# A third row buffer in front of the DOWN stage, and eight more unsplit units in the MID stage, of a one-core decoder block with PEER retrieval

## The chip, the cores and the metric

The kernel runs on one core of a Trainium2 chip. The metric is the device time of one launch in microseconds (us), lower is better; the median over several launches is compared.

## What is computed

One decoder block on 256 tokens of width 2048: a mixer (differential attention beside a causal convolution), then a feed-forward part that looks up single-neuron experts. Only the second part matters here:

```python
def peer_ffn(h, w_q, k1, k2, u_tab, v_tab):       # 256 tokens, 16384 experts, D = 2048
    q = (h @ w_q).reshape(T, 8, 256)              # 8 heads
    s1, s2 = q[..., :128] @ k1.T, q[..., 128:] @ k2.T
    v1, i1 = top_k(s1, 16); v2, i2 = top_k(s2, 16)
    top, pos = top_k(v1[:, None] + v2[None, :], 16)   # 16 experts for each head and token
    idx, g = i1 * 128 + i2 at pos, softmax(top)
    act = gelu(einsum('thkd,td->thk', u_tab[idx], h)) * g
    return einsum('thk,thkd->td', act, v_tab[idx])
```

All of it is float32.

## The kernel before

**Two ways to one sum.** The first 192 tokens take the dense way: TensorE multiplies their activations with the whole table u (128 blocks of 128 experts, 1 MB each), a gelu follows, a matrix of gates ("weights", in DRAM, filled by small accumulating DMAs) picks what counts, and the stage DOWN multiplies with the whole table v. For the last 64 tokens the 16 chosen experts of 8 heads are gathered as rows: 64 gathers ("rows" from here on) of 128 lines of 8 KB each, 1 MB per gather, first from u and later from v.

**Stages.** The dense part runs in the stages UP, MID, THIRD and LAST over u (32 blocks each, in 4 passes of 8 blocks, the first pass written out and the other three in a hardware loop), then DOWN over v. A block is two units of 8 k-chunks. A *split* unit is done in two parts of reduced-precision products: ScalarE rounds the unit to `w_hi` (L713), VectorE makes the rest `w_low` (L1382), TensorE runs eight matmuls with `w_hi` (L1008) and eight with `w_low` (L1015). A *plain* unit goes to TensorE as it is (L1001, sixteen records for eight matmuls), with no work on ScalarE or VectorE. Only MID has plain units, six of the sixteen in each pass (j = 1, 3, 7, 9, 11, 15). MID is also the last stage in which VectorE selects the top 16 (`experts`).

**Blocks of u and v.** SyncE brings them into `raw`, a ring of four blocks (L352): block b is asked for when both units of block b-4 are used (`split_used`). `w_hi` has two buffers; ScalarE fills one when TensorE has done the `w_hi` matmuls of the split unit two before (`hi_used`).

**Rows of u.** GpSimd issues the gathers (L491) into `got[0]` and `got[1]`, which the code takes in turn; the gather of row n waits for `row_used` n-1, that is for row n-2 to be done with. Behind each gather it issues the small DMAs that add gates to `weights` (`put_weights`, L506): 4, 4 and 3 in turn behind rows 1 to 15, and 2, 2, 2, 2, 1 in turn behind the later ones. VectorE takes each row's dot product with the token in two halves (L1403) between its `w_low` units (`dots_at`, called from `lo`): 4 rows in a pass of MID (16 in all), 6 in a pass of THIRD and of LAST (48 in all). A half waits for the row's DMA (`row_in`), and everything behind it in VectorE's order waits with it.

**The turn to DOWN.** SyncE, in the callback `weights_first`, behind the first block of v: waits for all `weights_put`, then loads the first two groups of gates back (`weights_group`, L390, 384 KB each) into `weights_in[0]` and `weights_in[1]`, two tiles of their own. The further blocks of v are behind that in its order. VectorE multiplies the first group into the activations (`make_group`, L1846), ScalarE and VectorE split it (L918, L1853, L1855), and only then can DOWN's first matmul run (L1339). The same wait for `row_used` 63 and 64 stands on GpSimd in front of the first two rows of v.

Of the kernel before, what the change touches and what calls it, by code (L numbers as in the profile page):

```python
# [6 lines left out]
P = 128  # L7
D = 2048
T = 256
TD = 192  # L10
# [20 lines left out]
UNIT = 1024  # L31
# [5 lines left out]
EXPERT_BLOCKS = KEYS  # L37


def at(i, step, first):  # L40

    return first if i is None else i * step + first
# [28 lines left out]

PH_WQ = Phase(None, BLOCKS // 4, 8)
PH_UP = Phase(PH_WQ, EXPERT_BLOCKS // 32, 16, groups=tuple(range(22, 30)))
PH_MID = Phase(PH_UP, EXPERT_BLOCKS // 32, 16, plain=(1, 3, 7, 9, 11, 15), groups=(30, 31, 4, 11, 12, 13, 14, 15))
PH_THIRD = Phase(PH_MID, EXPERT_BLOCKS // 32, 16, groups=(5, 6, 7, 8, 9, 10, 16, 17))
PH_LAST = Phase(PH_THIRD, EXPERT_BLOCKS // 32, 16, groups=(0, 1, 2, 3, 18, 19, 20, 21))
PH_DOWN = Phase(PH_LAST, EXPERT_BLOCKS // 8, 16)
U_ORDER = [4 * g + i for ph in (PH_UP, PH_MID, PH_THIRD, PH_LAST) for i in range(4) for g in ph.groups]
assert sorted(U_ORDER) == list(range(EXPERT_BLOCKS))
# [18 lines left out]
B_END = B_UP + EXPERT_BLOCKS  # L98
GROUPS = EXPERT_BLOCKS // 4
ROWS = PEER_HEADS * TOPK // SLICES  # L100
DOTS_MID_FIRST, DOTS_MID = tuple(range(8, 16)), (1, 2, 5, 6, 9, 10, 13, 14)
DOTS_ROUTE = (0, 1, 3, 4, 5, 6, 8, 9, 11, 12, 13, 14)
N_MID, N_ROUTE = len(DOTS_MID) // 2, len(DOTS_ROUTE) // 2
DOT_ROWS = {PH_MID: 0, PH_THIRD: N_MID * PH_MID.n, PH_LAST: N_MID * PH_MID.n + N_ROUTE * PH_THIRD.n}
assert DOT_ROWS[PH_LAST] + N_ROUTE * PH_LAST.n == ROWS and N_MID % 2 == N_ROUTE % 2 == 0
PUTS_SECOND, PUTS_FIRST = PEER_HEADS * TOPK // 2, PEER_HEADS * TOPK
PUTS = PUTS_SECOND + PUTS_FIRST
HEAD_ROWS = ROWS // PEER_HEADS
# [11 lines left out]
ALU = mybir.AluOpType  # L120
# [4 lines left out]
def build_block(nc, x, c, c_row, w_ada, w_gate_f, b_cols, g_cols, rows, w_front, lambdas, g_subln, conv_w,  # L125
                conv_vecs, peer_wq, peer_keys, peer_u, u_rows, peer_v, v_rows, out):
    with ExitStack() as ctx:
        def sb(name, shape, dt=F32):
            return ctx.enter_context(nc.sbuf_tensor(name, shape, dt))

        def sem(name):
            return ctx.enter_context(nc.semaphore(name))
# [8 lines left out]
        def region(start, *shape):  # L141
            n = int(math.prod(shape))
            v = big[:, start:start + n]
            if len(shape) == 2:
                v = v.rearrange("p (a b) -> p a b", b=shape[1])
            if len(shape) == 3:
                v = v.rearrange("p (a b c) -> p a b c", b=shape[1], c=shape[2])
            return v
# [36 lines left out]
        h_tok = region(28672, D)  # L185
# [27 lines left out]
        with nc.sbuf_tensor("early", [P, 5 * D], F32) as early:  # L213
# [12 lines left out]
        got = [region(24576 + n * D, D) for n in range(2)] + [early[:, 3072 + n * D:3072 + (n + 1) * D] for n in range(2)]  # L226
# [17 lines left out]
        put = sel[:, 0:2 * PUTS].rearrange("p (m n) -> p m n", m=2)  # L244
        put_at = sel[:, 0:PUTS].bitcast(U32)
        put_gate = sel[:, PUTS:2 * PUTS]
        weights_in = (sb("weights_in0", [P, 4, TD]), sb("weights_in1", [P, 4, TD]))
        token = sb("token", [P, 2])
        row_info = sb("row_info", [P, 2, ROWS])
        row_gate, row_ix = row_info[:, 0, :], row_info[:, 1, :].bitcast(U32)  # L250
        dots, row_act = sb("dots", [P, ROWS]), sb("row_act", [P, ROWS])
        dots_now = sb("dots_now", [P, N_ROUTE, 2])
        pair = sel[:, 2 * PUTS:2 * PUTS + TD]
        low = sb("low", [P, TD], F32R)
        ident_r = sb("ident_r", [P, P], F32R)
# [59 lines left out]
        at_made = sem("at_made")  # L315
        twice_made, h_turned, h_tok_made = sem("twice_made"), sem("h_turned"), sem("h_tok_made")
        picked_ready, row_info_in = sem("picked_ready"), sem("row_info_in")
        row_in = [sem(f"row_in{n}") for n in range(2)]
        v_row_in = [sem(f"v_row_in{n}") for n in range(4)]
        row_used, v_row_used, dots_put, row_gelu, row_act_made = (sem("row_used"), sem("v_row_used"), sem("dots_put"),  # L320
                                                                  sem("row_gelu"), sem("row_act_made"))
# [20 lines left out]
        def _(sp):  # L342
# [44 lines left out]
            def weights_group(g, i):  # L387

                src = weights[:, bass.ds(at(i, 8 * TD, 4 * TD * g), 4 * TD)]
                sp.dma_start(weights_in[g % 2][:, :, :].rearrange("p a t -> p (a t)"), src)\  # L390
                    .then_inc(weights_back[g % 2], 16)

            def weights_first(j, i):

                if j == 1:
                    sp.wait_ge(weights_put[0], 16 * PUTS_FIRST)
                    sp.wait_ge(weights_put[1], 16 * PUTS_SECOND)
                    weights_group(0, None)
                    weights_group(1, None)
                if j == 11:  # L400
                    sp.wait_ge(at_made, 1)
                    weights_group(2, None)
# [31 lines left out]
            for it in range(PH_WQ.n):  # L434
                bring(PH_WQ, it or None, peer_wq, 0, gate_loads)
            for ph, w, block0 in ((PH_UP, peer_u, 0), (PH_MID, peer_u, EXPERT_BLOCKS // 4),
                                  (PH_THIRD, peer_u, EXPERT_BLOCKS // 2), (PH_LAST, peer_u, 3 * EXPERT_BLOCKS // 4)):
                bring(ph, None, w, block0, gate_last if ph is PH_UP else None)
                with sp.Fori(1, ph.n) as i:
                    bring(ph, i, w, block0)  # L440
            bring(PH_DOWN, None, peer_v, 0, weights_first)
            with sp.Fori(1, PH_DOWN.n - 1) as i:
                bring(PH_DOWN, i, peer_v, 0, weights_next)
            bring(PH_DOWN, PH_DOWN.n - 1, peer_v, 0, weights_last)

            for n in range(4):
                tt, half = n // 2, slice((n % 2) * UNIT, (n % 2 + 1) * UNIT)
# [6 lines left out]
        def _(gp):  # L454
# [35 lines left out]
            def gather(n, table, where, done):  # L490
                gp.indirect_dma_start(where, None, table, bass.IndirectOffsetOnAxis(ap=row_ix[:, n:n + 1], axis=0))\  # L491
                    .then_inc(done, 16)
# [17 lines left out]
                put_weights(m)  # L510
            gp.wait_ge(gate_f_saved, 16)
            for n in range(ROWS):
                if n >= 2:
                    gp.wait_ge(row_used, n - 1)
                if n % HEAD_ROWS == 0:
                    gp.wait_ge(row_info_in, 16 * SLICES * (n // HEAD_ROWS + 1))
                gather(n, u_rows, got[n % 2], row_in[n % 2])
                for m in range(PUTS_AT[n], PUTS_AT[n + 1]):
                    put_weights(m)
            for n in range(ROWS):  # L520
# [11 lines left out]
        def _(act):  # L532
# [355 lines left out]

            for j in range(PH_MID.per):
                up_unit(PH_MID, j, None)  # L890
                if j == 2:
# [42 lines left out]
            high_group(0, None, 1)  # L934
            gelu(PH_DOWN, -1, None)
            hi(PH_DOWN, 1, None)
            act.wait_ge(dots_put, PH_MID.n + PH_THIRD.n + PH_LAST.n)
            act.activation(dots[:, :], dots[:, :], ACT.Gelu).then_inc(row_gelu, 1)
            down(None)
            with act.Fori(1, PH_DOWN.n - 1) as i:  # L940
# [425 lines left out]
        def _(dve):  # L1366
# [11 lines left out]
            def lo(ph, j, i):  # L1378
                s, h = ph.s + j, ph.nth(j)
                if j not in ph.plain:  # L1380
                    dve.wait_ge(hi_ready, ph.count(j, i))
                    dve.tensor_tensor(w_low[:, s % RING, :], raw[:, s % RING, :], w_hi[:, h % 2, :].bitcast(F32),  # L1382
                                      ALU.subtract).then_inc(lo_ready, 1)
                if ph is PH_MID:
                    dots_at(ph, j, i, DOTS_MID if i is not None else DOTS_MID_FIRST, N_MID, 0)
                if ph is PH_THIRD or ph is PH_LAST:
                    dots_at(ph, j, i, DOTS_ROUTE, N_ROUTE, PH_MID.n + (PH_THIRD.n if ph is PH_LAST else 0))

            def dots_at(ph, j, i, halves, per, before):

                if j not in halves:
                    return
                n, half = halves.index(j) // 2, halves.index(j) % 2
                first = DOT_ROWS[ph]
                buf, cols = (first + n) % 2, slice(half * UNIT, (half + 1) * UNIT)
                if half == 0:
                    dve.wait_ge(row_in[buf], at(i, 16 * per // 2, 16 * ((first + n) // 2 + 1)))
                if n == 0 and half == 0:
                    if i is not None or before:
                        dve.wait_ge(dots_put, at(i, 1, before))  # L1400
                    else:
                        dve.wait_ge(h_tok_made, 4)
                d = dve.tensor_tensor_reduce(got[buf][:, cols], got[buf][:, cols], h_tok[:, cols], 1.0, 0.0, ALU.mult,  # L1403
                                             ALU.add, dots_now[:, n, half:half + 1])
                if half:
                    d.then_inc(row_used, 1)
                if j == halves[-1]:
                    many = len(halves) // 2
                    dve.wait_ge(row_used, at(i, per, first + many))
                    dve.tensor_tensor(dots[:, bass.ds(at(i, per, first), many)], dots_now[:, 0:many, 0],  # L1410
                                      dots_now[:, 0:many, 1], ALU.add).then_inc(dots_put, 1)

            def gate_f_step(n):

# [182 lines left out]
            for g in range(4):  # L1597
                cols = slice(g * 512, (g + 1) * 512)
# [35 lines left out]
            def wq_lo(u):  # L1634
                lo(PH_WQ, u % PH_WQ.per, u // PH_WQ.per or None)
# [381 lines left out]
```

## Time and profile before

| | |
|---|---|
| three runs | 1813.8, 1822.11, 1822.92 us; median 1822.11 |
| the profiled execution | 1819.46 us, of which 1817.7 from the first to the last instruction (the span) |
| busy share of the span | TensorE 97%, VectorE 84%, ScalarE 44%, GpSimd 32% |
| granted TensorE clock, mean | 0.994 |
| moved by DMA | 617.22 MB, 340 GB/s over the span |

The stages in the profiled execution, from the first matmuls of each: UP 557 to 722 us, MID 722 to 894.5, THIRD and LAST 894.5 to 1219, DOWN from 1219 to 1803. A busy TensorE is not proof that it sets the time: it counts a wait inside a matmul group partly as busy. The mean DMA share is the time that packets took over the time of the 16 DMA engines; it can pass 1.00 where packets of two queues overlap on one engine.

### The profile page before, as it was taken

The numbers are of one execution on the slowest core, as the hardware profiler recorded it, in microseconds if no ns is written. First come the engines' busy times: TensorE is split into PE (matmuls) and PEld (weight loads), VectorE is DVE, ScalarE is ACT, GpSimd is POOL, SyncE is SP. The second block draws the span as 40 slices with busy tenths as digits, with TensorE's granted clock in tenths as the row PEclk, the third lists the DMA queues.
The fourth block names the chain that finished last, engine by engine and source line by source line (L and its number), as shares of the span: only waits on it lengthen the run. The fifth ranks groups of instructions, "written<-read, shape, count | busy, mean of one in ns | idle before, by whom it ended". The sixth has DMA issues, their size and how long they took to land.

```text
span 1817.7 us, 27824 instructions
## 1 busy us (share of the span) xinstructions
PE 1765.6 (97%) x9580; PEld 1536.2 (85%) x9580; DVE 1520.5 (84%) x2421; ACT 800.7 (44%) x1163; POOL 574.9 (32%) x388
## 2 busy tenths in 40 slices
PE   7999999999999999999999999999999999999998
PEld 6888888545999999989989999988888888888886
DVE  4669899967778999899978888878888888888887
ACT  3011222302635656444445555555554555555554
POOL 1000000111000488787677777741111111111110
PEclk9999999999999999999999999999999999999999
DMA  9999976799686688899999999999999999999994
GB/s 381 420 421 422 421 295 250 269 422 399 241 325 241 205 216 220 302 304 304 309 355 346 360 382 361 367 388 380 384 357 379 363 373 361 372 371 371 365 375 206
DMA packets 123723, 617.22 MB, mean 340 GB/s; under 512 B 42850, under 2 KB 43394, under 8 KB 52098
## 3 DMA queue, kind: packets, MB, share of 16 engines
q1 hardware_dynamic: 64258, 426.81, 61.1%
q0 software_dynamic: 53056, 184.69, 29.1%
q10 hardware_dynamic: 6338, 4.80, 0.8%
q8 instruction: 42, 0.69, 0.1%
q14 instruction: 29, 0.24, 0.0%
HBM read 599.22 MB, written 16.88 MB: 339 GB/s over the span
## 4 chain that ended last, share of the span: by engine, by line
PE 60%; DMA 13%; DVE 12%; POOL 7%; issue 6%; ACT 1%; DVEq 0%; SPq 0%; ACTq 0%; POOLq 0%
PE ps L1339 32%; DMA big<-in_u_rows,row_info 6%; PE ps L1175 5%; PE ps L1059 5%; PE ps L1008 5%; DMA raw<-in_w_ada 5%; POOL weights L506 5%; PE ps L1229 4%; PE ps L1015 3%; DVE big L1403 3%; PE ps L1070 2%; DVE w_low L1382 2%; POOL big L491 2%; DMA big<-in_w_gate_f 1%; DVE raw L1428 1%
## 5 line engine op out<-in xcount | busy, mean ns | idle before, releaser
L713 ACT ACTIVATE w_hi<-raw 128x1024 fp32r<-128x1024 f32 x520 | 550.9, 1060 | 515.9 <-PE ps L1339 240.5
L1382 DVE TENSOR_TENSOR w_low<-raw,w_hi 128x1024 fp32r<-128x1024 f32 x520 | 631.5, 1221 | 103.8 <-ACT w_hi L713 95.0
L506 POOL DMA_INDIRECT weights<-sel x192 | 358.7, 1868 | 239.4 <-DVE sel L1804 181.2
L1339 PE MATMUL ps<-w_hi,a 128*128 128x512 f32 x1536 | 390.0, 389 | 0.3 <-issue 0.3
L1008 PE MATMUL ps<-a,w_hi 128*128 128x384 f32 x1856 | 376.2, 344 | 0.8 <-issue 0.8
L1339 PEld LDWEIGHTS ps<-w_hi,a 128*128 128x128 f32 x1536 | 288.1, 188 | 60.6 <-issue 0.5
L1008 PEld LDWEIGHTS ps<-a,w_hi 128*128 128x128 f32 x1856 | 320.6, 191 | 1.6 <-issue 1.6
L1339 PE MATMUL ps<-w_low,a 128*128 128x512 f32 x1024 | 274.0, 389 | 0.0
L1015 PE MATMUL ps<-a,w_low 128*128 128x192 f32 x1856 | 245.8, 275 | 25.9 <-DVE w_low L1382 25.4
L1015 PEld LDWEIGHTS ps<-a,w_low 128*128 128x128 f32 x1856 | 238.3, 192 | 38.1 <-DVE w_low L1382 37.1
L1339 PEld LDWEIGHTS ps<-w_low,a 128*128 128x128 f32 x1024 | 192.0, 188 | 40.5 <-DVE w_low L1382 0.7
L1403 DVE CUSTOM_DVE_ANT_0 big<-big 128x1024 f32<-128x1024 f32 x128 | 156.2, 1220 | 51.2 <-DMA big<-in_u_rows,row_info 40.3
L1428 DVE CUSTOM_DVE_ANT_0 raw<-raw,big 128x2048 f32<-128x2048 f32 x64 | 146.0, 2289 | 55.7 <-DMA raw<-in_w_ada 55.7
L484 POOL DMA_DIRECT2D raw<-in_w_ada x48 | 25.4, 530 | 395.5 <-DVE macc L1428 223.6
L491 POOL DMA_INDIRECT big<-in_v_rows,row_info x32 | 44.9, 1403 | 243.4 <-DVE big L1881 214.9
L491 POOL DMA_INDIRECT big<-in_u_rows,row_info x64 | 93.0, 1453 | 83.2 <-DVE dots_now L1403 72.5
L491 POOL DMA_INDIRECT early<-in_v_rows,row_info x32 | 44.9, 1402 | 226.7 <-DVE big L1881 224.4
L1043 PE MATMUL ps<-big,early 128*128 128x256 f32 x512 | 111.9, 380 | 3.7 <-ACT big L562 3.7
L1059 PE MATMUL ps<-big,early 128*128 128x256 f32 x512 | 113.2, 380 | 0.2 <-DMA early<-in_w_front 0.2
L1043 PEld LDWEIGHTS ps<-big,early 128*128 128x128 f32 x512 | 96.8, 190 | 18.6 <-issue 5.7
L1175 PE MATMUL ps<-early,big 128*128 128x512 f32 x256 | 111.0, 592 | 0.0
L1059 PEld LDWEIGHTS ps<-big,early 128*128 128x128 f32 x512 | 96.3, 190 | 14.1 <-issue 1.6
(223 smaller groups left out, 1682.0 us busy)
## 6 DMA issues: line engine op xcount, KB each, us to landing
raw<-in_peer_u SPq DMA_DIRECT2D x128, 1024.0 KB
raw<-in_peer_v SPq DMA_DIRECT2D x128, 1024.0 KB
early<-in_w_front SPq DMA_DIRECT2D x56, 1024.0 KB, 11.7
raw<-in_w_ada POOLq DMA_DIRECT2D x48, 1024.0 KB, 9.5
raw<-in_w_ada SPq DMA_DIRECT2D x32, 1024.0 KB, 12.6
raw<-in_peer_wq SPq DMA_DIRECT2D x16, 1024.0 KB
big<-in_w_gate_f SPq DMA_DIRECT2D x16, 1024.0 KB, 7.1
weights<-weights_in SPq DMA_DIRECT2D x16, 768.0 KB, 19.1
```

Of the source, the lines that this page charges most:

```text
L491: gp.indirect_dma_start(where, None, table, bass.IndirectOffsetOnAxis(ap=row_ix[:, n:n + 1], axis=0))\
L506: gp.indirect_dma_start(weight_elements, bass.IndirectOffsetOnAxis(ap=put_at[:, c:c + 1], axis=0), put_gate[:, c:c + 1], None, compute_op= ...
L713: act.activation(w_hi[:, h % 2, :], raw[:, s % RING, :], ACT.Copy).then_inc(hi_ready, 1)
L1008: done = pe.matmul(ps[:, b % 2, 0:2 * TD].rearrange("p (m t) -> p m t", m=2), w_hi[:, ph.nth(j) % 2, k * P:(k + 1) * P], a_pair[:, kc, :, ...
L1015: done = pe.matmul(ps[:, b % 2, 0:TD], w_low[:, s % RING, k * P:(k + 1) * P], a_hi[:, kc, 0:TD], start=False, stop=False, skip_group_check ...
L1043: done = pe.matmul(ps[:, b // 2, (b % 2) * T:(b % 2 + 1) * T], w_slots[n % SLOTS][:, b * P:(b + 1) * P], hT[:, k, :], start=k == 0 and b % ...
L1059: done = pe.matmul(ps[:, e % 2, 0:T], w_slots[n % SLOTS][:, kc * P:(kc + 1) * P], hT[:, kc, :], start=kc == 0, stop=kc == KC - 1)
L1175: done = pe.matmul(ps[:, (MIX_FIRST, MIX_SECOND)[half][bank], :], mixed(place)[:, tt * P:(tt + 1) * P], w_slots[n % SLOTS][:, cols:cols + ...
L1339: done = pe.matmul(ps[:, 4 * tt + 2 * (j % 2) + n, :], a, w[:, n * 512:(n + 1) * 512], start=i is None and blk == 0 and m in (0, 2), stop= ...
L1382: dve.tensor_tensor(w_low[:, s % RING, :], raw[:, s % RING, :], w_hi[:, h % 2, :].bitcast(F32), ALU.subtract).then_inc(lo_ready, 1)
L1403: d = dve.tensor_tensor_reduce(got[buf][:, cols], got[buf][:, cols], h_tok[:, cols], 1.0, 0.0, ALU.mult, ALU.add, dots_now[:, n, half:half ...
L1428: dve.tensor_tensor_reduce(mod_slots[n % SLOTS], mod_slots[n % SLOTS], c_all, 1.0, 0.0, ALU.mult, ALU.add, macc[:, group, k:k + 1]).then_i ...
```

## The change

Three things. (1) In THIRD and LAST the rows go round three buffers, `third`, `got[0]`, `got[1]`; in MID they keep the two. The gather of row n from row 16 on waits for the last row in the same buffer, row n-3. (2) `third` is one tile of 2048 columns, and the two `weights_in` tiles become views of it; so `weights_first` has to wait on SyncE for all 64 rows to be used before it loads the groups. (3) Units j = 5 and 13 of each MID pass become plain, eight units in all. How many rows each pass holds is as before.

```diff
-PH_MID = Phase(PH_UP, EXPERT_BLOCKS // 32, 16, plain=(1, 3, 7, 9, 11, 15), groups=(...))
+PH_MID = Phase(PH_UP, EXPERT_BLOCKS // 32, 16, plain=(1, 3, 5, 7, 9, 11, 13, 15), groups=(...))
...
+THREE_FROM = DOT_ROWS[PH_THIRD]
+ROW_BUF = [n % 2 if n < THREE_FROM else (2, 0, 1)[(n - THREE_FROM) % 3] for n in range(ROWS)]
+ROW_NTH = [ROW_BUF[:n + 1].count(ROW_BUF[n]) for n in range(ROWS)]
...
-        weights_in = (sb("weights_in0", [P, 4, TD]), sb("weights_in1", [P, 4, TD]))
+        third = sb("third", [P, D])
+        weights_in = [third[:, n * 4 * TD:(n + 1) * 4 * TD].rearrange("p (a t) -> p a t", t=TD) for n in range(2)]
...
                     sp.wait_ge(weights_put[1], 16 * PUTS_SECOND)
+                    sp.wait_ge(row_used, ROWS)
                     weights_group(0, None)
...
             for n in range(ROWS):
-                if n >= 2:
-                    gp.wait_ge(row_used, n - 1)
+                if ROW_NTH[n] > 1:
+                    gp.wait_ge(row_used, max(m for m in range(n) if ROW_BUF[m] == ROW_BUF[n]) + 1)
...
-                gather(n, u_rows, got[n % 2], row_in[n % 2])
+                gather(n, u_rows, (got[0], got[1], third[:, :])[ROW_BUF[n]], row_in[ROW_BUF[n]])
```

In `dots_at` the buffer and the count waited for on `row_in` follow from these tables; the instructions that it issues are the same.

## Rows read from the trace of the kernel before

**Rows 1.** Windows: busy time by engine in MID's passes, THIRD with LAST, DOWN.
```profile
core 0: us, PE busy (x) PEld busy (x) DVE busy (x) ACT busy (x) POOL busy (x), PEclk, DMA share, GB/s
722.00:762.00 40.00, 39.67 (x266) 39.30 (x265) 36.06 (x114) 17.89 (x29) 29.03 (x18) 1.00 0.92 311
762.00:810.20 48.20, 42.72 (x268) 40.90 (x266) 42.22 (x125) 18.13 (x29) 41.31 (x23) 0.96 0.87 287
810.20:852.40 42.20, 40.55 (x267) 39.24 (x265) 39.11 (x119) 18.13 (x29) 31.18 (x21) 1.00 0.93 301
852.40:894.50 42.10, 40.43 (x266) 39.11 (x265) 39.13 (x119) 18.97 (x30) 25.93 (x18) 1.00 0.91 300
894.50:1219.00 324.50, 309.94 (x2111) 306.59 (x2111) 264.44 (x337) 171.21 (x258) 231.76 (x131) 0.98 1.01 363
1219.00:1803.00 584.00, 583.65 (x2582) 482.60 (x2581) 509.58 (x485) 298.77 (x298) 87.00 (x62) 1.00 0.95 364
```

**Rows 2.** Timeline of PE: two starts of the same unit, one block apart, LAST.
```profile
1162.21 1.59 PE L1008 MATMUL ps<-a,w_hi 128*128 128x384 f32 x8
...
1166.91 0.36 PE L1008 MATMUL ps<-a,w_hi 128*128 128x384 f32 x1
```

**Rows 3.** Waits in 894.5 to 1219 us: total, times, longest.
```profile
POOL big L491 <- DVE dots_now L1403: 59.8, 25, 6.7
DVE big L1403 <- DMA big<-in_u_rows,row_info: 35.4, 22, 4.3
PEld ps L1015 <- DVE w_low L1382: 17.6, 10, 3.0
```

**Rows 4.** Timeline of POOL and DVE: a gather, what follows, its wait.
```profile
941.86 1.00 POOL L491 DMA_INDIRECT big<-in_u_rows,row_info  x1 [0.30 <-issue]
943.16 1.57 POOL L506 DMA_INDIRECT weights<-sel  x1 [0.31 <-issue]
...
948.19 1.74 POOL L491 DMA_INDIRECT big<-in_u_rows,row_info  x1 [1.14 <-DVE dots_now L1403]
...
951.53 1.23 DVE L1403 CUSTOM_DVE_ANT_0 big<-big 128x1024 f32<-128x1024 f32 x1 [2.47 <-DMA big<-in_u_rows,row_info]
```

**Rows 5.** DMA queues in 894.5 to 1219 us: packets, MB, share of engines.
```profile
DMA packets 28861, 117.82 MB, mean 363 GB/s; under 512 B 14336, under 2 KB 14336, under 8 KB 14592
...
q1 hardware_dynamic: 9408, 67.24, 53.8%
q0 software_dynamic: 18864, 50.38, 46.6%
```

**Rows 6.** Windows: the first loads, and 38 us twice inside THIRD and LAST.
```profile
33.00:56.00 23.00, 23.00 (x108) 20.26 (x107) 14.56 (x19) 1.80 (x3) 0.00 (x0) 1.00 1.01 422
...
1046.00:1084.00 38.00, 37.14 (x262) 36.82 (x261) 31.88 (x41) 20.56 (x32) 27.38 (x17) 1.00 1.04 380
970.00:1008.00 38.00, 36.00 (x243) 35.68 (x241) 30.57 (x39) 19.22 (x29) 28.01 (x17) 0.96 0.99 347
```

**Rows 7.** Timeline of PE: two split units of MID, one plain unit between.
```profile
857.71 1.69 PE L1008 MATMUL ps<-a,w_hi 128*128 128x384 f32 x8
...
862.71 1.71 PE L1008 MATMUL ps<-a,w_hi 128*128 128x384 f32 x8
```

**Rows 8.** The w_low units of one MID pass: min/median/max ns.
```profile
L1382 DVE TENSOR_TENSOR w_low<-raw,w_hi x10: 1224/1226/1247, 810.7 to 847.5; 128x1024 fp32r<-128x1024 f32 x10
```

**Rows 9.** Timeline of the turn to DOWN, by engine: DVE, SP, PE.
```profile
1213.35 1.22 DVE L1403 CUSTOM_DVE_ANT_0 big<-big 128x1024 f32<-128x1024 f32 x1 [3.71 <-DMA big<-in_u_rows,row_info]
...
1216.79 0.08 DVE L1403 DVE_READ_ACCUMULATOR2_ANT dots_now<- 128x1 f32 x1
...
1218.32 0.94 DVE L1846 TENSOR_TENSOR big<-big,weights_in 128x768 f32<-128x768 f32 x1
...
1209.66 1.02 SPq L390 DMA_DIRECT2D weights_in<-weights  x2
1210.73 20.83 SPq L352 DMA_DIRECT2D raw<-in_peer_v  x5
...
1221.85 1.63 PE L1339 MATMUL ps<-w_hi,a 128*128 128x512 f32 x6 [0.34 <-issue]
```

More of the change, by code:

```diff
@@ L73 @@
 PH_UP = Phase(PH_WQ, EXPERT_BLOCKS // 32, 16, groups=tuple(range(22, 30)))
-PH_MID = Phase(PH_UP, EXPERT_BLOCKS // 32, 16, plain=(1, 3, 7, 9, 11, 15), groups=(30, 31, 4, 11, 12, 13, 14, 15))
+PH_MID = Phase(PH_UP, EXPERT_BLOCKS // 32, 16, plain=(1, 3, 5, 7, 9, 11, 13, 15), groups=(30, 31, 4, 11, 12, 13, 14, 15))
 PH_THIRD = Phase(PH_MID, EXPERT_BLOCKS // 32, 16, groups=(5, 6, 7, 8, 9, 10, 16, 17))
@@ L100 @@
 ROWS = PEER_HEADS * TOPK // SLICES
[L101 to L105, printed above, removed]
+FOUR_ROWS, SIX_ROWS = (1, 2, 5, 6, 9, 10, 13, 14), (0, 1, 3, 4, 5, 6, 8, 9, 11, 12, 13, 14)
+DOTS = {PH_MID: (tuple(range(8, 16)), FOUR_ROWS), PH_THIRD: (SIX_ROWS, SIX_ROWS), PH_LAST: (SIX_ROWS, SIX_ROWS)}
+DOT_ROWS, DOT_STEPS, first, steps = {}, {}, 0, 0
+for ph, (peeled, looped) in DOTS.items():
+    DOT_ROWS[ph], DOT_STEPS[ph] = first, steps if peeled else steps - 1
+    first += len(peeled) // 2 + (ph.n - 1) * len(looped) // 2
+    steps += (len(peeled) > 0) + ph.n - 1
+N_DOT_STEPS = steps
+assert first == ROWS
+THREE_FROM = DOT_ROWS[PH_THIRD]
+ROW_BUF = [n % 2 if n < THREE_FROM else (2, 0, 1)[(n - THREE_FROM) % 3] for n in range(ROWS)]
+ROW_NTH = [ROW_BUF[:n + 1].count(ROW_BUF[n]) for n in range(ROWS)]
 PUTS_SECOND, PUTS_FIRST = PEER_HEADS * TOPK // 2, PEER_HEADS * TOPK
@@ L251, in build_block @@
         dots, row_act = sb("dots", [P, ROWS]), sb("row_act", [P, ROWS])
-        dots_now = sb("dots_now", [P, N_ROUTE, 2])
+        dots_now = sb("dots_now", [P, len(SIX_ROWS) // 2, 2])
         pair = sel[:, 2 * PUTS:2 * PUTS + TD]
@@ L317, in build_block @@
         picked_ready, row_info_in = sem("picked_ready"), sem("row_info_in")
-        row_in = [sem(f"row_in{n}") for n in range(2)]
+        row_in = [sem(f"row_in{n}") for n in range(3)]
         v_row_in = [sem(f"v_row_in{n}") for n in range(4)]
@@ L936, in _ @@
             hi(PH_DOWN, 1, None)
-            act.wait_ge(dots_put, PH_MID.n + PH_THIRD.n + PH_LAST.n)
+            act.wait_ge(dots_put, N_DOT_STEPS)
             act.activation(dots[:, :], dots[:, :], ACT.Gelu).then_inc(row_gelu, 1)
@@ L1383, in lo, with dots_at @@
                                       ALU.subtract).then_inc(lo_ready, 1)
[L1384 to L1389, printed above, removed]
+                if ph in DOTS:
+                    dots_at(ph, j, i)
+            def dots_at(ph, j, i):
+                halves = DOTS[ph][0 if i is None else 1]
                 if j not in halves:
                     return
-                n, half = halves.index(j) // 2, halves.index(j) % 2
-                first = DOT_ROWS[ph]
-                buf, cols = (first + n) % 2, slice(half * UNIT, (half + 1) * UNIT)
+                n, half, per = halves.index(j) // 2, halves.index(j) % 2, len(halves) // 2
+                row = DOT_ROWS[ph] + (len(DOTS[ph][0]) // 2 if i is not None else 0)
+                first = row - (per if i is not None else 0)
+                buf, cols, steps = ROW_BUF[row + n], slice(half * UNIT, (half + 1) * UNIT), DOT_STEPS[ph]
+                in_loop = per // len(set(ROW_BUF[row:row + per]))
                 if half == 0:
-                    dve.wait_ge(row_in[buf], at(i, 16 * per // 2, 16 * ((first + n) // 2 + 1)))
+                    dve.wait_ge(row_in[buf], at(i, 16 * in_loop, 16 * (ROW_NTH[row + n] - (in_loop if i is not None else 0))))
                 if n == 0 and half == 0:
-                    if i is not None or before:
-                        dve.wait_ge(dots_put, at(i, 1, before))
-                    else:
-                        dve.wait_ge(h_tok_made, 4)
-                d = dve.tensor_tensor_reduce(got[buf][:, cols], got[buf][:, cols], h_tok[:, cols], 1.0, 0.0, ALU.mult,
+                    if steps < 0 or steps == 0 and i is None:
+                        dve.wait_ge(h_tok_made, 4)
+                    else:
+                        dve.wait_ge(dots_put, at(i, 1, steps))
+                here = (got[0], got[1], third)[buf][:, cols]
+                d = dve.tensor_tensor_reduce(here, here, h_tok[:, cols], 1.0, 0.0, ALU.mult,
                                              ALU.add, dots_now[:, n, half:half + 1])
@@ L1411, in dots_at @@
                                       dots_now[:, 0:many, 1], ALU.add).then_inc(dots_put, 1)
+                    if steps < 0:
+                        dve.wait_ge(dots_put, at(i, 1, steps + 1))
             def gate_f_step(n):
```

## The prediction

> **What bounds the kernel now.** I read the profile by stages first, because TensorE at 97% of the span says little about one stage. In the windows [rows 1] DOWN is filled by TensorE (583.65 of 584 us); the change touches nothing that runs inside it, so its 584 us stand. THIRD with LAST is different: 324.5 us for 64 blocks. The pace of TensorE where nothing holds it up is one block in 1166.91 - 1162.21 = 4.70 us [rows 2], so 64 blocks need 64 x 4.70 = 301 us. Some 23.5 us of the stretch are stalls.
>
> Whose stalls, the waits say [rows 3]: TensorE's weight loads wait for `w_low` 17.6 us, VectorE waits 35.4 us at dot products for the rows' DMA, and GpSimd waits 59.8 us at gathers for rows to be used up. That is a ring that is too short. One turn of it stands in the timeline [rows 4]: the gather of a row starts at 941.86, and its first half starts on VectorE at 951.53, 9.7 us later, after a wait of 2.47 us. A row takes 37.6 / 6 = 6.3 us at TensorE's pace (a pass is 8 x 4.70 us with 6 rows). With two buffers the gather can start when the row two before is used, which leaves it 6.3 us and the gap to the next dot; it takes up to 9.7. VectorE stands, the `w_low` units queued behind the dot product stand with it, then TensorE.
>
> But the same stretch has a second limit, close behind. It moves 117.82 MB [rows 5] with the DMA engines' share at 1.01 [rows 1]. In the windows [rows 6] the first loads show 422 GB/s when all is full. Inside the stretch, with the small DMAs of the gates between, a good 38 us gives 380 GB/s and a bad one 347. At TensorE's free pace the stretch would want 117.82 MB / 301 us = 391 GB/s.
>
> MID's last two passes are another case [rows 1]: VectorE is busy 39.1 of 42.2 us, with its waits for its own chain of selections in the rest, and TensorE waits for it.
>
> **Part one, the third buffer.** It removes the wait of a gather for the row two before. No instruction is added on GpSimd or VectorE, and GpSimd issues the same gathers and gates in the same order. A gather may start one row, 6.3 us, earlier; against the 9.7 us measured that covers the 2.5 to 4.3 us that VectorE waits today [rows 3, 4]. GpSimd can follow: 231.76 us busy plus 131 gaps of 0.3 us is 271 us [rows 1, 4], less than 301. VectorE has 264 us of work. So nothing but TensorE and the DMA engines is left as a limit: 301 us by the first; by the second 117.82 / 380 = 310 us with the good rate, and 117.82 / 363 = 324.5 us if the mean rate is all that is to be had. Which one? The bad windows are those in which the gathers were held back (TensorE's clock drops to 0.96 there after the stalls), and the good one has share 1.04 with only 0.9 us of TensorE idle, so I take 380 as the rate when requests are always there: 324.5 - 310 = **14.5 us gained**, between 0 and 23.5.
>
> The Trainium skill (DMA: Bandwidth & Descriptors, "Where 436 GB/s comes from") puts loads from HBM at some 358 GB/s per core and speaks against this part; by that rate the stretch would take 329 us, no less than now. Rows of this case pass it (422 and 380 GB/s) with one core at work, so I follow the rows. Its section "Issuing engines are not separate DMA queues" says that what SyncE and GpSimd issue shares the same 16 engines; the shares of the two queues, 53.8% and 46.6%, adding up to the full set [rows 5], agree.
>
> **Part two, plain units in MID.** Each pass loses two `w_low` units at 1.226 us [rows 8], 2.45 us of VectorE, and two roundings of ScalarE that hide under TensorE (18 busy of 42 us). TensorE pays: a split and a plain unit take 862.71 - 857.71 = 5.00 us [rows 7], so a pass of eight such pairs needs 40.0 us and can't be faster, whatever VectorE does. The last two passes thus go from 42.2 and 42.1 to 40.0: 4.3 us. The second pass takes 48.2 us; GpSimd is busy 41.31 us in 23 instructions with 0.3 us between, all of it, and its early rows come when GpSimd gets to them. Behind that VectorE is the limit again, so I count its 2.4 us, not the 8 down to the floor. The first pass is 40.0 already: 0. Sum **6.6 us gained**. The bounds: 0 if the gates hold up rows in the faster MID (4 gathers and 14.7 gates in a pass, at the second pass's 41.31 / 23 = 1.8 us and 0.3 between, are 39 us, close under 40), and 8 more if the second pass falls to its floor, which I don't expect.
>
> **Part three, the wait on SyncE.** `weights_first` waits today for the last gates and loads at 1209.66 [rows 9]. Now it waits for row 64 as well, which is used at 1216.87. Its last wait of 3.71 us goes if the rows are in time, so on today's clock the row is done at 1213.2; the group is asked for at 1213.5 instead of 1209.7, 3.8 us later. Queued behind it on SyncE: the second group and the next blocks of v, asked for at 1210.73 now and 1214.6 then. The waiters are VectorE's `make_group` and through it DOWN's first matmul, 1221.85 - 1218.32 = 3.5 us later. Without today's 1.5 us of TensorE idle before the last units, DOWN could begin at about 1220.3, so the group must be there at 1216.8. How long it takes to land is not shown; the nearest rows bound it: 1.9 us from the rate (0.79 MB for both groups at 422 GB/s) and 8.7 us from today's start to its use without a wait. The lower end costs nothing, the upper 1213.5 + 8.7 - 1216.8 = 5.4 us. I take 2 us, nearer the short side, since the load is small but the engines are full: **2 us lost**, with the blocks of v just in time, as the first is in the ring and the second is wanted 4.6 us into DOWN.
>
> **The sum.** 14.5 + 6.6 - 2 = 19.1 us. The profiled execution took 1819.46 us (span 1817.7, 1.8 around it), which gives 1800.4; it is 2.65 us under the median of the runs, so the median should be **1803 us**, 1.0% faster. A measurement of this kernel can tell some 0.5%, 9.1 us, from no change: faster is under 1813, slower over 1831.
>
> **The rivals.**
> - *TensorE's pace.* The DMA engines take the 391 GB/s, and the group lands in time: 23.5 + 6.6 = 30.1 us, 1792. For it: the first loads, without gates between them, reach 422 GB/s [rows 6]. Against: the gates' small packets, half of all packets, cost engine time. 0.15.
> - *MID gives nothing.* Gates on GpSimd hold the rows: 14.5 - 2, 1809.5. For it: the full GpSimd of the second pass; against: in the two later passes GpSimd has some 15 us to spare (84.3 us less 57.1 busy less 39 gaps of 0.3) [rows 1]. 0.12.
> - *The third buffer only moves the queue.* The engines are full at 363 GB/s, rows are late by as much as they were early asked for: 0 + 6.6 - 2, 1817.5, no change that can be told. For it: share 1.01. Against: 380 in a window with share 1.04, 347 in one with 0.99. 0.17.
> - *Slower: the blocks of u starve.* A queue that always has a row waiting takes half of the engines, and the blocks' queue gets 190 of 380 GB/s, a block in 5.5 us instead of 4.7: 64 x 0.8 = 51 us, if it held throughout; it can't, since rows are used up only as fast as blocks. If it held for half of the stretch, 26 us lost in place of 14.5 gained: 1822 + 26 - 6.6 + 2 = 1843. It decides once a block comes later than about 11 us after its request (it is asked for at the end of block b-4 and wanted 4.6 units of 2.35 us later); today no wait of ScalarE for a block stands among the stretch's waits. 0.04. The skill's "Queues, rings and completion order" of the same page has each engine take the queues in turn, which is the sharing that this would need.
>
> **How the numbers follow.** The forecast has 0.52. Faster: 0.52 + 0.15 + 0.12 = 0.79, less 0.01 for a forecast that falls short, 0.78; within 0.5%: 0.18; slower: 0.04. The range leaves out the slower case and most of the queue-only case, and takes in TensorE's pace: 1792 to 1815.
>
> **What would show it.** Right: in THIRD and LAST VectorE's wait for rows is under 10 us (35.4 now), the stretch is near 310 us at 375 to 385 GB/s, MID's last passes are 40 us each, and the first matmul of DOWN waits a little for the group. Wrong in part one: the same stretch with the rate still near 363, or ScalarE waiting for blocks of u. Wrong in part two: passes over 41 us with VectorE idle at rows. Wrong in part three: over 4 us between LAST's last unit and DOWN's first beyond the 3 of now.

## The result, and the profile after

The changed kernel takes 1792.34 us (median of 4 runs, 1790.71 to 1793.64), the kernel before 1822.51 (the three runs above and a fourth): ratio 0.9844, 95% interval 0.9812 to 0.9876, 1.6% faster. The forecast was 1803 with a range down to 1792. The profiled execution has a span of 1788.9 us; before it was 1817.7, so 28.8 us are to be found.

The windows of the changed kernel, cut at its own stages (four passes of MID, THIRD with LAST); the columns are those of [rows 1].

```profile
721.60:761.60 40.00, 40.00 (x266) 39.94 (x265) 33.36 (x112) 16.11 (x27) 28.12 (x18) 1.00 0.90 313
761.60:808.10 46.50, 42.65 (x267) 41.57 (x266) 40.90 (x124) 16.20 (x27) 39.48 (x24) 0.96 0.91 297
808.10:848.20 40.10, 40.10 (x267) 40.10 (x265) 37.14 (x120) 16.20 (x27) 34.31 (x20) 1.00 0.90 315
848.20:888.30 40.10, 40.10 (x266) 40.10 (x265) 37.02 (x117) 17.15 (x28) 34.01 (x21) 1.00 0.94 327
888.30:1189.70 301.40, 301.40 (x2114) 301.37 (x2114) 264.61 (x336) 170.64 (x258) 234.21 (x129) 1.00 1.03 386
```

THIRD with LAST went from 324.5 to 301.4 us, and TensorE is busy in all of them; that is the 64 blocks at 4.70 us of [rows 2]. The window before ends at 1219.0, but LAST's last unit ended at 1219.42 there: with these 0.4 us the stretch took 324.9 us, and the gain is 23.5. The granted clock is back at 1.00. MID went from 172.5 to 166.7: its last two passes are at 40.1 us each, filled by TensorE, and the second pass still has 6 us too many. So MID gives 5.8 us. Some 0.4 us were gained before MID began, and DOWN, from its first matmul on, took 596.7 us (1788.9 less 1192.2) instead of 595.8 (1817.7 less 1221.85 [rows 9]), 0.9 us lost. That accounts for the 28.8 us.

The waits in 888.3 to 1189.7 us (total, times, longest). Of the three rows of [rows 3], two have no successor: VectorE no longer waits for a row's DMA, nor TensorE's weight loads for `w_low`; only GpSimd waits for buffers, in the third line (and 3.3 us more in front of gathers into `third`), less than half as long as before.

```profile
ACT w_hi L722 <- PE ps L1017: 110.1, 108, 1.1
DVE w_low L1391 <- ACT w_hi L722: 31.4, 30, 1.2
POOL big L500 <- DVE dots_now L1414: 25.3, 9, 10.0
```

What is queued at the front now is TensorE: ScalarE waits for it, and VectorE for ScalarE. One row's way stands in the timelines of GpSimd and VectorE (start, length, instruction), to be laid beside [rows 4]:

```profile
943.67 1.44 POOL L500 DMA_INDIRECT big<-in_u_rows,row_info  x1 [0.30 <-issue]
945.41 1.57 POOL L515 DMA_INDIRECT weights<-sel  x1 [0.30 <-issue]
947.29 1.94 POOL L515 DMA_INDIRECT weights<-sel  x1 [0.30 <-issue]
949.53 1.00 POOL L500 DMA_INDIRECT third<-in_u_rows,row_info  x1 [0.30 <-issue]
...
955.99 1.22 DVE L1414 CUSTOM_DVE_ANT_0 big<-big 128x1024 f32<-128x1024 f32 x1
```

The gather of 943.67 is used at 955.99, 12.3 us later and without a wait; before, the gather of 941.86 was used 9.7 us later and after a wait. Here the gathers stand back to back with the gates. Over the whole stretch GpSimd still waits for a used row in front of ten gathers of u, 15.8 us in all, where it did so 24 times for 55.1 us before.

Laying every gather beside its first dot product gives the measure of the ring. Before, the 22 rows that VectorE waited for landed 7.4 to 11.1 us after the start of their gathers. In the changed kernel rows 17 to 63 have 12.0 to 15.0 us from gather to use, and none is waited for in this execution.

The turn to DOWN, in the timelines of SyncE, VectorE, TensorE and ScalarE:

```profile
1175.83 0.34 SPq L360 DMA_DIRECT2D raw<-in_peer_v  x1
1185.52 1.24 SPq L398 DMA_DIRECT2D third<-weights  x2
1186.81 10.54 SPq L360 DMA_DIRECT2D raw<-in_peer_v  x4
...
1189.01 0.96 DVE L1859 TENSOR_TENSOR big<-big,third 128x768 f32<-128x768 f32 x1 [2.06 <-DMA third<-weights]
...
1189.75 0.63 PE L1158 MATMUL ps<-ones,ident 128*128 128x128 f32 x4
...
1192.18 1.62 PE L1348 MATMUL ps<-w_hi,a 128*128 128x512 f32 x6 [0.35 <-issue]
...
1195.15 2.04 ACT L722 ACTIVATE w_hi<-raw 128x1024 fp32r<-128x1024 f32 x2 [2.83 <-DMA raw<-in_peer_v]
```

SyncE asks for the groups at 1185.52, as soon as row 64 is used, and the first is there 3.5 us later. VectorE waits 2.06 us for it, and yet DOWN's first matmul begins 2.43 us after the end of LAST's last unit (1189.75), which is the time it took before as well (1219.42 to 1221.85): the wait lies beside TensorE's own last units. The price shows further down, where ScalarE waits 2.83 us for the second block of v, which was queued on SyncE behind the groups.

### The profile page after: what moved, and what is told of

It is laid out like the page before. It is cut to its first block, busy times and chain, and to the rows that moved or that the text cites. A ratio compares the mean times of both kernels' runs of the same rounds, so it can differ in the third digit from the quotient of the medians.

```text
span 1788.9 us, 27787 instructions
## 1 busy us (share of the span) xinstructions
PE 1756.5 (98%) x9580; PEld 1533.6 (86%) x9580; DVE 1512.6 (85%) x2413; ACT 792.6 (44%) x1155; POOL 586.5 (33%) x388
## 4 chain that ended last, share of the span: by engine, by line
PE 80%; DMA 8%; DVE 6%; issue 3%; ACT 1%; POOL 1%; DVEq 0%; SPq 0%; ACTq 0%
PE ps L1348 32%; PE ps L1017 15%; PE ps L1024 9%; PE ps L1184 5%; PE ps L1068 5%; DMA raw<-in_w_ada 5%; PE ps L1238 4%; PE ps L1010 4%; PE ps L1079 2%; DVE raw L1441 1%; DMA early<-in_w_front 1%; DMA big<-in_w_gate_f 1%; DVE big L1497 1%; DMA raw<-in_peer_v 1%; POOL weights L515 1%
## 5 line engine op out<-in xcount | busy, mean ns | idle before, releaser
L722 ACT ACTIVATE w_hi<-raw 128x1024 fp32r<-128x1024 f32 x512 | 542.2, 1060 | 488.8 <-PE ps L1348 236.6
L1391 DVE TENSOR_TENSOR w_low<-raw,w_hi 128x1024 fp32r<-128x1024 f32 x512 | 624.1, 1224 | 127.3 <-ACT w_hi L722 117.3
L515 POOL DMA_INDIRECT weights<-sel x192 | 370.4, 1929 | 239.0 <-DVE sel L1817 180.7
L1017 PE MATMUL ps<-a,w_hi 128*128 128x384 f32 x1792 | 360.5, 342 | 0.8 <-issue 0.8
L1017 PEld LDWEIGHTS ps<-a,w_hi 128*128 128x128 f32 x1792 | 306.4, 189 | 1.6 <-issue 1.6
L1024 PEld LDWEIGHTS ps<-a,w_low 128*128 128x128 f32 x1792 | 229.8, 191 | 11.1 <-DVE w_low L1391 10.5
L1024 PE MATMUL ps<-a,w_low 128*128 128x192 f32 x1792 | 233.2, 272 | 6.1 <-DVE w_low L1391 5.8
L1414 DVE CUSTOM_DVE_ANT_0 big<-big 128x1024 f32<-128x1024 f32 x96 | 117.0, 1219 | 6.4 <-DMA big<-in_u_rows,row_info 5.6
L1184 PEld LDWEIGHTS ps<-early,big 128*128 128x128 f32 x256 | 48.4, 190 | 59.3 <-issue 59.2
```

Source lines behind the costliest of these rows:

```text
L515: gp.indirect_dma_start(weight_elements, bass.IndirectOffsetOnAxis(ap=put_at[:, c:c + 1], axis=0), put_gate[:, c:c + 1], None, compute_op= ...
L722: act.activation(w_hi[:, h % 2, :], raw[:, s % RING, :], ACT.Copy).then_inc(hi_ready, 1)
L1017: done = pe.matmul(ps[:, b % 2, 0:2 * TD].rearrange("p (m t) -> p m t", m=2), w_hi[:, ph.nth(j) % 2, k * P:(k + 1) * P], a_pair[:, kc, :, ...
L1024: done = pe.matmul(ps[:, b % 2, 0:TD], w_low[:, s % RING, k * P:(k + 1) * P], a_hi[:, kc, 0:TD], start=False, stop=False, skip_group_check ...
L1184: done = pe.matmul(ps[:, (MIX_FIRST, MIX_SECOND)[half][bank], :], mixed(place)[:, tt * P:(tt + 1) * P], w_slots[n % SLOTS][:, cols:cols + ...
L1414: d = dve.tensor_tensor_reduce(here, here, h_tok[:, cols], 1.0, 0.0, ALU.mult, ALU.add, dots_now[:, n, half:half + 1])
```

## The experiments

**One part at a time: the third buffer alone.**

```diff
-PH_MID = Phase(..., plain=(1, 3, 5, 7, 9, 11, 13, 15), ...)      # the changed kernel
+PH_MID = Phase(..., plain=(1, 3, 7, 9, 11, 15), ...)
```

> The changed kernel with MID's units as before (six plain ones in a pass). Theory 1: the third buffer is worth all of TensorE's stalls in THIRD and LAST, and the two parts don't touch each other: THIRD with LAST 301 to 302 us, MID 172.4 us as before, the median 22 to 24 us under that of the kernel before. Theory 2: part of the gain in THIRD and LAST needs the faster MID (rows and blocks that are further ahead at its end, so that the DMA engines start with an empty queue): the stretch takes 305 us or more.

1797.44 us, ratio 0.9864 (0.9846 to 0.9883). The windows of MID and of THIRD with LAST:

```profile
722.80:895.50 172.70, 162.87 (x1057) 158.66 (x1057) 156.51 (x476) 73.10 (x117) 133.04 (x81) 0.99 0.92 302
895.50:1197.00 301.50, 301.50 (x2116) 301.33 (x2114) 266.06 (x338) 170.66 (x258) 232.89 (x128) 1.00 1.03 385
```

Theory 1 holds in both lines, and the median is 23.0 us under that of the kernel before in these runs (1820.46), as it had it. The third buffer doesn't need the faster MID. VectorE waited for one row in the stretch, 0.4 us for one that landed 13.9 us after its gather: three buffers are enough here, without much to spare.

**The plain units alone,** in the kernel before.

```diff
-PH_MID = Phase(..., plain=(1, 3, 7, 9, 11, 15), ...)             # the kernel before
+PH_MID = Phase(..., plain=(1, 3, 5, 7, 9, 11, 13, 15), ...)
```

> The kernel before with eight more plain units in MID and two row buffers throughout. Theory 1: MID falls from 172.4 to 166.8 us, THIRD and LAST keep their 324.5 us, the median is 5.5 to 6.5 us under the kernel before, 0.3%. Theory 2 (rows in the faster MID come late when MID has no slack): MID over 169 us.

1811.69 us, ratio 0.9951 (0.993 to 0.9973).

```profile
722.50:888.80 166.30, 162.49 (x1058) 161.63 (x1057) 148.21 (x470) 65.71 (x109) 134.27 (x79) 0.99 0.93 311
888.80:1211.80 323.00, 308.30 (x2115) 303.40 (x2114) 263.82 (x337) 171.61 (x258) 228.41 (x130) 0.99 1.01 364
```

MID is 6.2 us shorter, as in the changed kernel; the two-buffer stretch behind it keeps its stalls (323.0 against 324.5 us). The median gives 8.8 us, more than the 5.5 to 6.5 of theory 1, with an interval that reaches down to 5. By the windows the parts add up: 6 and 23 us.

**How much the DMA engines carry.** The forecast had the stretch stop at 380 GB/s. Two loads of 512 KB more in each of three passes ask for more than the changed kernel does. Not shown here: SyncE also waits in front of these passes until the columns that it writes are free, and ScalarE waits in LAST until the loads have landed.

```diff
+            def extra_load(j, i):                      # on SyncE, passes 2 to 4 of THIRD
+                for at_j, base in ((3, 13824), (11, 0)):
+                    if j == at_j:
+                        sp.dma_start(big[:, bass.ds(i * 1024 + base - 1024, 1024)], peer_u[at_j][:, 0:1024])
```

> The changed kernel with two loads more of 512 KB in each of the last three passes of THIRD, into columns that nothing uses at that time; what is computed is unchanged. It asks for 15.7 MB in a pass, 418 GB/s at TensorE's pace of 37.6 us. Theory 1 (the engines with the gates between carry some 400 GB/s, so the changed kernel at 391 is just under the limit): the three passes take 39.3 us each, 5 us more in all, and ScalarE waits for blocks of u. Theory 2 (the 380 GB/s of the forecast was the engines' limit with queues full, and the changed kernel passes it only in small part): 41.4 us each, 11 us more. Theory 3 (422 GB/s are to be had, the gates cost nothing): no change.

1796.98 us (2 runs, ratio 0.9865), by the ratios some 4 us over the changed kernel. The three passes:

```profile
927.60:1043.30 115.70, 113.72 (x794) 112.72 (x793) 98.61 (x124) 63.99 (x97) 88.30 (x50) 1.00 1.06 411
```

They took 115.7 us, against 113.0 for the same 48 units in the changed kernel, 2.8 us more for 3.1 MB more, and moved 411 GB/s with the gates between (the changed kernel 394). The trace lies between theory 1 (5 us more) and theory 3 (none). Whether 418 GB/s are beyond the engines is not shown: the last of the three passes (1005 to 1043 us) moved 414 GB/s with TensorE busy throughout. What became late was mostly the other side from what was expected, as the waits of 927 to 1045 us show: VectorE waited for rows, in both kinds of buffer, 6.8 us in all; ScalarE waited for a block of u once.

```profile
DVE big L1427 <- DMA big<-in_u_rows,row_info: 3.9, 2, 3.1
PEld ps L1037 <- DVE w_low L1404: 2.9, 3, 1.5
DVE third L1427 <- DMA third<-in_u_rows,row_info: 2.9, 2, 2.3
...
ACT w_hi L734 <- DMA raw<-in_peer_u: 1.4, 1, 1.4
```

The four rows waited for had landed 13.2 to 18.9 us after the start of their gathers, against 7.4 to 11.1 us in the kernel before at 363 GB/s. That is beyond much of the 12.0 to 15.0 us that three buffers give.

**Are the gates to blame for the late rows?** The kernel before, two buffers, without the 85 gate DMAs behind rows 16 to 63. These gates are left out of the result, and SyncE's wait for the gates at the turn to DOWN is lowered to those that are left (not shown here).

```diff
-                for m in range(PUTS_AT[n], PUTS_AT[n + 1]):
+                for m in range(PUTS_AT[n], PUTS_AT[n + 1] if n < 16 else PUTS_AT[n]):
                     put_weights(m)
```

> The kernel before with none of the small gate DMAs that stand behind rows 16 to 63 (85 of 192); the gates of the last heads are missing from the result. Theory 1: the stalls of THIRD and LAST are the short ring of two buffers: a gather of 1 MB in the midst of the blocks takes some 8 us with or without gates, against 6.3 us and the gap to the next row; without gates it is issued at once and lands 1 or 2 us earlier, so 5 to 15 of the 23 us of stalls stay. Theory 2: gates on GpSimd and in the DMA engines are what makes the rows late, and two buffers would be enough without them: THIRD with LAST 301.5 us.

1824.2 us, ratio 1.0012 (0.9994 to 1.0029): no change at all. The window and the waits of 894.5 to 1222 us:

```profile
894.50:1222.00 327.50, 310.30 (x2114) 305.15 (x2113) 264.72 (x338) 171.59 (x258) 77.10 (x49) 0.98 0.95 358
```

```profile
POOL big L491 <- DVE dots_now L1403: 259.3, 49, 9.6
...
DVE big L1403 <- DMA big<-in_u_rows,row_info: 50.1, 27, 4.6
```

GpSimd stands idle for 259 us with nothing to do but to wait for a used row, and VectorE waits 50 us for rows, more than the 35 of [rows 3]. Theory 2 is out, and theory 1 had too small a number: it expected that 5 to 15 of the 23 us of stalls stay, and all of them stay. With two buffers it is the ring, whatever stands between the gathers. The rate is 358 GB/s with a share of 0.95: in this stretch the rate followed from the stalls, not the stalls from the rate.

**SyncE's wait alone,** in the kernel before.

```diff
                     sp.wait_ge(weights_put[1], 16 * PUTS_SECOND)
+                    sp.wait_ge(row_used, ROWS)
```

> The kernel before with SyncE's wait for all 64 rows added in front of the first groups, and nothing else changed (two row buffers, two tiles for the groups). It prices part three of the change alone, at its dearest, since row 64 is late there. The forecast's step: the group is asked for at 1216.9 instead of 1209.7 us, needed at 1218.3, so DOWN's first matmul comes 2 to 7 us later. The theory from the changed kernel's trace: a group lands 3.0 us after it is asked for, so the first matmul is 1 to 2 us late, and the blocks of v that are queued behind cost up to 4 us more: the median 2 to 6 us over the kernel before.

1822.28 us, ratio 1.0005 (0.9989 to 1.0021): within what can't be told from no change, under the 2 to 6 us of both expectations. In the trace the first matmul of DOWN (1219.19) starts 2.43 us after LAST's last unit (1216.76), with no delay. But row 64 was not late in that execution: it was used at 1212.43, 4.3 us before the last unit's end, as in the changed kernel (1185.42 and 1189.75), where the kernel before had 2.6. So the run gives the price of the wait with the row in time, and not the dearest case that was meant. ScalarE then waits twice for blocks of v:

```profile
1224.69 2.01 ACT L714 ACTIVATE w_hi<-raw 128x1024 fp32r<-128x1024 f32 x2 [5.36 <-DMA raw<-in_peer_v]
1229.66 2.01 ACT L714 ACTIVATE w_hi<-raw 128x1024 fp32r<-128x1024 f32 x2 [2.96 <-DMA raw<-in_peer_v]
```

DOWN is 3.1 us longer in that execution (span 1818.1 less 1219.2 is 598.9, against 595.8). So the wait seems to have a price, not where the forecast put it, and of a size that the medians don't resolve.

**The groups behind the second block of v,** in the changed kernel.

```diff
-                if j == 1:
+                if j == 3:
                     sp.wait_ge(weights_put[0], 16 * PUTS_FIRST)
```

> The changed kernel with SyncE's wait for the gates and the 64 rows, and the loads of the first two groups, behind the second block of v instead of behind the first. Theory 1: the wait costs nothing in front of DOWN's first matmul but makes the second and third block of v late (ScalarE waits for them 2.8 and 2.3 us just behind it, TensorE's DOWN is 596.7 us long instead of 595.8, and 599 to 600 in two other runs with the same wait); with one block more in front, the waits of ScalarE for the second block go and DOWN takes 595.8 to 597 us; the median falls by 0 to 3 us, to 1789 to 1792. Theory 2: the group lands later behind a whole block, and DOWN's first matmul comes 2 us or more later: median 1793 to 1796.

1791.76 us, ratio 0.9838 (0.9814 to 0.9862), the same as the changed kernel's 0.9844. ScalarE's waits for blocks of v at the start of DOWN are gone (one of 3.42 us near its end stands in both kernels), and DOWN's first matmul has one instead, 1.14 us where it had 0.35:

```profile
1193.41 0.93 PE L1348 MATMUL ps<-w_hi,a 128*128 128x512 f32 x3 [1.14 <-issue]
```

DOWN takes 596.5 us, and the median is at the upper end of theory 1's 1789 to 1792; the price that theory 2 named is there too, but 0.8 us instead of 2 or more. The one wait was traded for the other.

**The gates behind rows 1 to 3.** What is left in MID is the second pass, 46.5 us instead of 40.1. In the changed kernel GpSimd issues the gather of row 2 at 743.45, four gates, row 3 at 753.75, three gates, row 4 at 761.31, without a pause; row 4's place in VectorE's order comes up at 767.1, and it waits 2.5 us. In front of row 2 GpSimd has waited for 7.0 us.

```diff
-PUTS_BEHIND = [0] + [4, 4, 3] * 5 + [2, 2, 2, 2, 1] * 10
+PUTS_BEHIND = [0, 7, 2, 2] + [4, 4, 3] * 4 + [2, 2, 2, 2, 1] * 10
```

> The changed kernel with the small DMAs of the gates spread otherwise behind rows 1 to 3 of MID: 7, 2 and 2 instead of 4, 4 and 3, in the same order and number. Theory 1: the second pass of MID is 46.5 us long instead of 40.1 because GpSimd issues 7 gates between rows 2 and 4 and rows 3 and 4 are late by that; with them moved in front, where GpSimd waits 7 us anyway, the pass takes 40.1 to 41 us and the median falls by 5.5 to 6.5 us to some 1786. Theory 2: the two buffers of MID set those waits, since a row can't be asked for before the one two before is used: row 4 then comes at most 1 or 2 us earlier, and the median stays at 1790 to 1792.

1786.58 us, ratio 0.9809 (0.9792 to 0.9826). GpSimd's timeline, and the second pass in the windows:

```profile
744.52 1.00 POOL L500 DMA_INDIRECT big<-in_u_rows,row_info  x1 [1.05 <-DVE dots_now L1414]
...
749.99 1.00 POOL L500 DMA_INDIRECT big<-in_u_rows,row_info  x1 [0.32 <-DVE dots_now L1414]
...
756.35 1.00 POOL L500 DMA_INDIRECT big<-in_u_rows,row_info  x1 [1.27 <-DVE dots_now L1414]
```

```profile
762.50:804.00 41.50, 40.66 (x266) 39.92 (x265) 38.35 (x119) 16.21 (x27) 35.41 (x21) 1.00 0.96 319
```

Row 4 is asked for 33.9 us after the start of MID instead of 39.7, and the pass takes 41.5 us instead of 46.5. That is theory 1, with a pass half a microsecond longer than its 40.1 to 41 us.

**Both of these.**

> The gates spread as 7, 2, 2 behind rows 1 to 3 and the groups behind the second block of v. If both act on places of their own: MID 161.8 us, DOWN 595.8 to 597 us instead of 599.5, the median 1 to 4 us under the kernel with the gates alone (1786.6), at 1783 to 1786. If the block in front of the groups makes the first matmul of DOWN late: 1787 or more.

1788.34 us, ratio 0.9814 (0.9792 to 0.9837): the gates' gain and nothing on top. The first matmul of DOWN had a wait of 1.67 us in front of it, so it is the second case of the expectation.

**The changed kernel and the one with the gates moved, in the same rounds.**

> The changed kernel once more, unaltered, on the same chip and in the same rounds as the kernel with the gates spread as 7, 2, 2. It gives the distance between the two without the kernel before as a go-between: ratio to the kernel before 0.983 to 0.985.

> The kernel with the gates spread as 7, 2, 2, once more. If the gain in MID's second pass (46.5 to 41.5 us in the traces) is real and nothing takes it back, the median is 3 to 6 us under that of the changed kernel of the same rounds. If DOWN's late blocks of v take it back (599.5 instead of 596.7 us in the one trace), it is 1 to 3 us under.

1791.78 us (0.9844, 0.9817 to 0.987) and 1785.92 us (0.981, 0.9784 to 0.9836): 5.9 us between the medians, as in the first comparison. All six runs with the gates moved (up to 1789.78) are faster than all six of the changed kernel (from 1791.44), so that version beats both kernels.

## Why the prediction was right, and where it was off

The direction and the mechanisms were right, the size was not: 19 us forecast, 30 measured by the medians, 28.8 by the spans. The time is that of the first rival, TensorE's pace, which had a chance of 0.15, to within 1 us, and at the very edge of the range. Point by point:

- *What bounds the stretch* was right: the ring of two buffers. It is shown from both sides, by the third buffer alone (301.5 us) and by the gates taken away with two buffers kept (327.5).
- *Part one, the term that was mis-sized:* 14.5 us forecast, 23.5 measured, in the step "I take 380 as the rate when requests are always there". The window of 380 GB/s [rows 6] was the better of two windows of a stretch that stalls, and it was read as what could be had. The changed kernel moves 386 GB/s over the whole stretch, 394 in three passes of it, and the one with more loads 411 over 116 us. The share of 1.01 [rows 1] was read as "full"; it stands at 1.03 and at 1.06 in those two, with more moved.
- *The rule that spoke against it,* some 358 GB/s per core for loads from HBM (the Trainium skill, DMA: Bandwidth & Descriptors, "Where 436 GB/s comes from"), is not borne out here: the rows show 386 and 411 GB/s, with one core at work.
- *The rival that only the queue moves* (0.17) falls by the same numbers. *The starving blocks* (0.04) fall too: in the changed kernel ScalarE waits for no block of u in the stretch, and even with 411 GB/s on the engines it does so once, for 1.4 us, while rows come late by 6.8 us.
- *Part two:* 6.6 forecast, 5.8 measured. The floor of 40.0 us for a pass of eight pairs was met in the last two (40.1). The second pass gave 1.7 us, where I had counted 2.4, the two `w_low` units; why it fell short by 0.7 was not tried. That most of its 6.4 us rest lay in GpSimd's queue is shown by the gates moved in front of row 2, which take 5.0 us of it away.
- *Part three:* 2 us lost forecast, 0.9 found, and in another place. The group is used 3.5 us after SyncE asks for it, near the short end of the bounds, in time for the first matmul. What the wait delays are the blocks of v behind it, which the forecast had "just in time". In other executions with the same wait DOWN is 0 to 4 us longer (596.2 and 599.5 in the two with the gates moved, 599.8 with the third buffer alone). The length goes with one block: where ScalarE begins the second block of v 7.8 to 8.3 us after SyncE starts to ask for it (the changed kernel twice, the gates moved in one of two), DOWN takes 596.2 to 596.7 us; where it is 10.8 to 10.9 us, after a wait of 5.4 us (the third buffer alone, the wait alone, the gates moved in the other), 598.9 to 599.8. Why the block takes longer in some executions stays open.
- *MID gives nothing* (0.12) is out: the gates held no row back in the two later passes.

## What to carry to other kernels

A rate seen in a stretch that stalls is what the stalls let through: before taking it for the engines' limit, look whether it falls as the stalls grow, and let the upper bound be the best rate of the whole trace (here 422 GB/s, not 380). A ring is long enough when the time from asking to use, at the free pace of the engine that sets the end, exceeds the measured landing time. Here a third buffer raised that time to 12.0 to 15.0 us, against landing times of 7.4 to 11.1 us. The landing time moves too: with loads added it went up to 18.9 us and the waits came back, so leave a margin over what the stalled stretch shows. And where several kinds of DMA share an issuing queue, put the filler where the queue waits anyway, not in front of the load that is waited for.

## What the runs showed of the hardware that was not expected

The share of the DMA engines can stand at 1.00 while 18% more can be moved: 347 GB/s at 0.99 [rows 6], 386 at 1.03, 411 at 1.06, with the same kinds of packets. Nor does it take two queues to pass 1.00, as the section on the profile before has it: in 33 to 56 us [rows 6] a single queue moves everything, with a share of 101.3%. Taking away 85 of the small accumulating DMAs changed neither the rate nor the time to speak of (358 against 363 GB/s), though GpSimd's busy time in the stretch fell from 231.8 to 77.1 us. And a 1 MB gather has no landing time of its own: the rows waited for landed in 7.4 to 11.1 us at 363 GB/s with two buffers, one in 13.9 us at 385 with three, and four in 13.2 to 18.9 us at 411 with three. Whether the higher rate or the gathers queued one behind the other lengthen it was not separated.
